# A third k-tile pair of eight goes to the 7-product scheme in the up projections of a fused encoder block

## The reference

```
h = x + 0.5 * swiglu(rms_norm(h), w_gate, w_up, w_down)       # FFN 1, hidden width 5632
...                                                           # combined projection, two attentions, gates, w_out
h = h + 0.5 * swiglu(rms_norm(h), w_gate, w_up, w_down)       # FFN 2, hidden width 5632
...                                                           # per-layer embedding, final norm
swiglu(x, wg, wu, wd) = (silu(x @ wg) * (x @ wu)) @ wd
```

## Time and profile before

| | |
|---|---|
| time, median of 3 runs | 2249.02 us (2248.64 to 2249.76) |
| profiled execution, its own time | 2249.12 us |
| span in the profile, first to last instruction | 2247.1 us |
| PE busy | 2217.0 us (99% of the span), 9950 instructions |
| DVE busy | 1337.5 us (60%) |
| ACT busy | 1050.7 us (47%) |
| DMA | 425.66 MB, mean 189 GB/s |
| mean granted TensorE clock | 0.995 |

### The profile page before, as it was taken

The page is one execution under the profiler, slowest core; times in us unless marked ns, Lnnn a source line. Parts: engine busy times, 40 slices in busy tenths (PEclk is TensorE's granted clock), DMA queues, the critical chain, the costliest instruction groups (busy, mean ns, idle before and its releaser), DMA issues.

```text
span 2247.1 us, 24310 instructions
## 1 busy us (share of the span) xinstructions
PE 2217.0 (99%) x9950; PEld 1827.4 (81%) x9950; DVE 1337.5 (60%) x1318; ACT 1050.7 (47%) x1147; POOL 40.4 (2%) x71
## 2 busy tenths in 40 slices
PE   8999999999999999999999998899999999999998
PEld 7888888888888888877778887788878888888886
DVE  5777544677555444445655654777754467755555
ACT  6445434454444444464444443454543345544454
POOL 0000000000010000010000000000000000000000
PEclk9999999999999999999999999999999999999999
DMA  8455456555465666665655664555546664556654
GB/s 312 177 202 205 164 196 205 207 186 191 175 201 187 198 195 190 175 179 173 174 168 159 187 187 143 213 172 203 207 149 191 204 221 171 197 178 212 187 189 147
DMA packets 161079, 425.66 MB, mean 189 GB/s; under 512 B 11320, under 2 KB 11328, under 8 KB 143568
## 3 DMA queue, kind: packets, MB, share of 16 engines
q1 hardware_dynamic: 159216, 419.21, 57.3%
q0 software_dynamic: 1472, 4.70, 0.8%
q10 hardware_dynamic: 288, 0.30, 0.0%
HBM read 422.06 MB, written 2.11 MB: 189 GB/s over the span
## 4 chain that ended last, share of the span: by engine, by line
PE 97%; DMA 1%; DVE 1%; ACT 0%; issue 0%; ACTq 0%; POOLq 0%; POOL 0%
PE acc L1470 18%; PE acc L1472 18%; PE acc L1471 18%; PE acc L1513 6%; PE acc L1515 6%; PE acc L1514 6%; PE turn L1515 4%; PE turn L1513 4%; PE turn L1514 4%; PE fox L1515 4%; PE fox L1514 4%; PE fox L1513 4%; DMA raw<-in_ffn_up 1%; PE turn L1490 1%; PE acc L1507 0%; PE turn L1762 0%
## 5 line engine op out<-in xcount | busy, mean ns | idle before, releaser
L1003 DVE TENSOR_TENSOR w_lo<-raw,w_hi 128x1024 fp32r<-128x1024 f32 x451 | 557.9, 1240 | 604.0 <-ACT w_hi L573 603.6
L573 ACT ACTIVATE w_hi<-raw 128x1024 fp32r<-128x1024 f32 x451 | 477.0, 1060 | 704.0 <-PE acc L1472 633.9
L1470 PE MATMUL acc<-w_hi,x_both 128*128 128x512 f32 x940 | 370.7, 394 | 2.8 <-DVE x_both L1165 2.8
L1472 PE MATMUL acc<-w_hi,x_both 128*128 128x512 f32 x940 | 366.3, 390 | 0.0
L1471 PE MATMUL acc<-w_lo,x_both 128*128 128x512 f32 x940 | 365.9, 389 | 0.0
L1470 PE MATMUL acc<-w_hi,slab_r 128*128 128x512 f32 x832 | 325.9, 392 | 2.6 <-DVE w_lo L1003 2.6
L1472 PE MATMUL acc<-w_hi,slab_r 128*128 128x512 f32 x832 | 324.5, 390 | 0.0
L1471 PE MATMUL acc<-w_lo,slab_r 128*128 128x512 f32 x832 | 324.4, 390 | 0.0
L1058 DVE TENSOR_TENSOR w_lo<-raw,w_hi 128x2048 fp32r<-128x2048 f32 x84 | 192.2, 2290 | 100.8 <-ACT w_hi L629 100.3
L629 ACT ACTIVATE w_hi<-raw 128x2048 fp32r<-128x2048 f32 x84 | 161.2, 1919 | 191.1 <-PE fox L1515 93.5
L1470 PEld LDWEIGHTS acc<-w_hi,x_both 128*128 128x128 f32 x940 | 176.5, 188 | 44.8 <-issue 5.7
(11 more groups left out here) (368 smaller groups left out, 3200.9 us busy)
## 6 DMA issues: line engine op xcount, KB each, us to landing
raw<-in_ffn_up SPq DMA_DIRECT2D x88, 1024.0 KB, 4.9
raw<-in_ffn_w_down SPq DMA_DIRECT2D x176, 512.0 KB
raw<-in_w_in SPq DMA_DIRECT2D x96, 512.0 KB
more<-in_ffn_up SPq DMA_DIRECT2D x46, 1024.0 KB, 4.9
raw<-in_w_merge_gate SPq DMA_DIRECT2D x64, 512.0 KB
raw<-in_ffn_up SPq DMA_DIRECT2D x37, 512.0 KB, 4.0
raw<-in_w_out SPq DMA_DIRECT2D x32, 512.0 KB
raw<-in_w_ple_gate SPq DMA_DIRECT2D x32, 512.0 KB
```

What stands on the lines that cost most here:

```text
L573: nc.scalar.activation(w_hi[:, slot, :, :], raw[:, slot, :, :], ACT.Copy).then_inc(hi_split, 1)
L1003: nc.vector.tensor_tensor(w_lo[:, slot, :, :], raw[:, slot, :, :], w_hi[:, slot, :, :].bitcast(F32), ALU.subtract).then_inc(lo_split, 1)
L1470: nc.tensor.matmul(to, hi(kt)[:, tok], w_hi[:, slot, k, :], start=kt == 0, stop=False)
L1472: last = nc.tensor.matmul(to, lo(kt)[:, tok], w_hi[:, slot, k, :], start=False, stop=kt == BK * nb - 1)
```

## The change

`US` goes from 2 to 3: of the eight units of a pair, three are A and B items. A middle stage now reads B0 S3 B1 S4 A0' B2 S5 A1' S6 A2' S7.

Room for it is made by sharing. Raw weights and low parts are in one ring of five buffers (`tall`: `raw` twice, `w_lo` twice, `more` once): the low part is written over the raw weights. High parts have four quads. The B tiles (`later_tiles`) are also split in place; for unit 2 they lie in `corner`, where POOL's masks and `thin_rows` lie later, and in one tile of `more`. So a raw buffer is free for a load only when PE has multiplied what was in it. The wait of L392 is gone. `make_sums` and `split_sums` go a unit at a time through `m1_copy` and `m5_copy`. `copy_parts` and `combine` stand behind the first item of a stage and no longer behind the last one of the stage before. POOL makes its masks later.

```diff
-US = 2
-QUADS = 3
+US = 3
+QUADS = 4
+TALL = 5
...
 def stage_of(pair, first, pairs):
     own = [("S", pair, u) for u in range(UNITS)]
     if pair > first:
-        own = [("B", pair, 0), own[US], ("B", pair, 1), *own[US + 1:]]
+        b0, b1, b2 = [("B", pair, u) for u in range(US)]
+        own = [b0, own[US], b1, own[US + 1], b2, *own[US + 2:]]
     if pair + 1 < pairs:
-        later = [("A", pair + 1, u) for u in range(US)]
-        own = [*own[:-2], *later, *own[-2:]]
+        a0, a1, a2 = [("A", pair + 1, u) for u in range(US)]
+        own = [*own[:4], a0, *own[4:6], a1, own[6], a2, own[7]]
     return own
...
-        quad_free, raw_free, trio_free = [b0 - 2, b0, early], [b0 - 2, b0, early], [early] * US
-        order, quad, slot, at, made = ((0, 1, 2) if name == "up2a" else (2, 0, 1)), 0, 0, b0, []
+        kinds = [kind for p in range(first, pairs) for kind, _, _ in stage_of(p, first, pairs)]
+        quads = [(i - len(kinds)) % QUADS for i in range(len(kinds))]
+        whole = UNITS * (pairs - first)
+        slots = [(r - whole) % TALL for r in range(whole)]
+        if name == "up2a":
+            quads[0], slots[0:2] = 0, (0, 1)
+        quad_free, trio_free = [b0 - 2, b0, early, early], [early] * US
+        raw_free, raw_split = [0, 0, b0 - 2, b0, early], [b0 - 2, b0, 0, 0, 0]
...
-                if up == "up2a":
-                    sp.wait_ge(multiplied, BLOCK[up])
...
-                        if it.kind != "B" and it.raw_free > 0:
-                            sp.wait_ge(lo_split, it.raw_free)
+                        if it.kind != "B":
+                            if it.raw_split > 0:
+                                sp.wait_ge(lo_split, it.raw_split)
+                            if it.raw_free > 0:
+                                sp.wait_ge(multiplied, it.raw_free)
...
                         if it.kind == "A":
-                            sp.dma_start(raw_quad(up, it.raw)[:, 0:3:2, :], source[:, 0:2, :]).then_inc(quad_full[it.raw], 16)
-                            sp.wait_ge(lo_split, it.trio_free)
-                            sp.dma_start(trio(up, it.unit)[:, 0:2, :], source[:, 2:4, :]).then_inc(trio_full[it.unit], 16)
+                            sp.dma_start(tall(up, it.raw, 0)[:, 0:3:2, :], source[:, 0:2, :]).then_inc(tall_full[it.raw], 16)
+                            sp.wait_ge(multiplied, it.trio_free)
+                            sp.dma_start(later_tiles(up, it.unit, 0)[0][:, 0:2, :], source[:, 2:4, :])\
+                              .then_inc(trio_full[it.unit], 16)
...
-                        if k == 1 and n == 0:
-                            if later_rows:
-                                later_rows()
-                            if sums is not None:
-                                make_sums(name, hi, lo, sums)
-                        if k == 3 and n == 0 and sums is not None:
-                            split_sums(sums)
+                        if k == 1 and n == 0 and later_rows:
+                            later_rows()
+                        if 2 <= k <= 4 and n == 0 and sums is not None:
+                            split_sums(k - 2, sums)
+                        if 1 <= k <= 3 and n == 0 and sums is not None:
+                            make_sums(k - 1, hi, lo, sums)
```

More of the change, by code:

```diff
@@ L49 @@
 UNITS = KD // BK
-US = 2
-QUADS = 3
+US = 3
+QUADS = 4
+TALL = 5
 DOWN_OF = {"up1a": "down1a", "up1b": "down1b", "up2a": "down2a", "up2b": "down2b"}
 BEFORE = {"up1a": "up1a", "up1b": "down1a", "up2a": "up2a", "up2b": "down2a"}
-Item = namedtuple("Item", "kind pair unit at quad quad_free raw raw_free raw_count trio_free trio_count step")
+Item = namedtuple("Item", "kind pair unit at quad quad_free raw raw_free raw_split raw_count trio_free trio_count step")
 def stage_of(pair, first, pairs):
@@ L108, in item_tables @@
 def item_tables(block):
-    counts, steps, stages, after = {"raw": [0] * QUADS, "trio": [0] * US}, 0, {}, {}
+    counts, steps, stages, after = {"raw": [0] * TALL, "trio": [0] * US}, 0, {}, {}
     for name, (pairs, first) in UPS.items():
@@ L133, in item_tables @@
                     trio_free[u] = at + 1
-                stage.append(Item(kind, pair, u, at, q, quad_free[q], raw, r_free, r_count, t_free, t_count, step))
+                stage.append(Item(kind, pair, u, at, q, quad_free[q], raw, r_free, r_split, r_count, t_free, t_count, step))
                 quad_free[q] = at + 1
@@ L138, in item_tables @@
         stages[name] = made
-        after[block[DOWN_OF[name]]] = (raw_free, quad_free)
+        split_after = [max(quad_free[n], raw_free[2 + n]) for n in range(2)]
+        after[block[DOWN_OF[name]]] = (raw_free[0:2], split_after)
     return stages, after
@@ L362, in slot_free @@
             def slot_free(blk):
-                sp.wait_ge(lo_split, raw_after(blk))
+                first = blk - blk % RING
+                if first in AFTER:
+                    sp.wait_ge(multiplied, AFTER[first][0][blk % RING // 2])
+                else:
+                    sp.wait_ge(lo_split, blk - RING + 1)
             def load(blk, src):
@@ L620, in split_item @@
             def split_item(name, it):
-                n = 3 if it.kind == "B" else 4
-                of = trio(name, it.unit) if it.kind == "B" else raw_quad(name, it.raw)
                 if it.kind == "S":
-                    act.wait_ge(quad_full[it.raw], 16 * it.raw_count)
+                    act.wait_ge(tall_full[it.raw], 16 * it.raw_count)
                 if it.kind == "A":
@@ L628, in split_item @@
                 act.wait_ge(multiplied, it.quad_free)
-                nc.scalar.activation(hi_quad(name, it.quad)[:, 0:n, :], of[:, 0:n, :], ACT.Copy)\
-                    .then_inc(hi_split, item_counts(name, it))
+                at = 0
+                for of in raw_parts(name, it):
+                    n = of.shape[1]
+                    last = nc.scalar.activation(hi_quad(name, it.quad)[:, at:at + n, :], of, ACT.Copy)
+                    at += n
+                last.then_inc(hi_split, item_counts(name, it))
             def copy_parts(name, pair):
@@ L654, in up_phase @@
                         split_item(name, it)
+                        if k == 0 and n > 0:
+                            copy_parts(name, pair)
                         if k == 1 and pair > 0:
@@ L1517, in multiply_item @@
             def multiply_item(name, it, hi, lo, primed, last_unit, ready):
-                banks, whole, rest = banks_of(name, it.pair), hi_quad(name, it.quad), lo_quad(name, it.quad)
+                banks, whole = banks_of(name, it.pair), hi_quad(name, it.quad)
+                rest = [part[:, n, :] for part in lo_parts(name, it) for n in range(part.shape[1])]
                 first, second = BK * it.unit, BK * it.unit + 1
@@ L1559, in up_groups @@
                             pe.wait_ge(turned_lo, TURN[name] + 2 * pair)
-                            if sums is not None and n == 0:
-                                pe.wait_ge(sums_lo, sums)
+                        if it.kind == "A" and sums is not None and n == 0:
+                            pe.wait_ge(sums_lo, sums - US + it.unit + 1)
                         def ready(ct):
```

162 lines of the change are left out of this document (81 added, 81 removed).

## The result

| | before | changed |
|---|---|---|
| time, median (lowest to highest), 6 runs each | 2249.39 us (2248.64 to 2249.89) | 2257.62 us (2255.91 to 2258.51) |
| profiled execution, its own time | 2249.12 us | 2255.91 us |
| span | 2247.1 us | 2253.8 us |
| mean granted TensorE clock | 0.995 | 0.998 |

The changed kernel is slower: ratio 1.0036, 95% interval 1.0025 to 1.0047. Forecast were 2243.2 us and "faster", so the time lies inside the range of 2230 to 2268, and the sign is wrong. (The profiled execution is the fastest of the changed kernel's six; between the medians +8.2 came.)

A forecast was written before the change was run, and what follows sets the result against it. The prediction took PE, holding 97% of the chain that ended last, as the bound. Its terms, -11.6 + 19.6 - 10.7 - 4.4 + 1.2 = -5.9 against 2249.1, gave 2243.2 us, range 2230 to 2268.

The forecast's parts named there:

- Matmuls: All on PE's path: 17 pairs lose 3 matmuls each, 51 at 0.2268 us, -11.6 us.
- Middle stages: 13 stages: new PE waits in front of S4 (0.65) and S6 (0.75 plus 0.1), 1.5 us each, +19.6 us.
- Landing of the second half: Middle stages: the 512 KB load of A's second half lands in 3.7 us, near bounds 3.4 and 4.1.
- slower landing: Rival, middle stages: loads issued right behind share the DMA engines, landing 4.6 to 4.9, +27, 2270 us; chance 0.17.
- The restart: Middle stages, at S6: 0.1 us extra for PE restarting without a running pipeline.
- Start of up2a: FFN 2: of 15.7 us lost before, 5.0 stays, as S0's load is issued several blocks ahead; -10.7 us.
- Turn to down2a: FFN 2: block 0's quad is free 11 us earlier, so the 4.4 us lost before go; -4.4 us.
- Start of up1a: First stage: more sums on DVE make S3 ready at 71.4 for PE at 71.0, S4 0.7 late; +1.2 us.
- the main case: The summed forecast with landing between 3.4 and 4.1, 2235 to 2254 us; chance 0.60, of it 0.03 slower.
- The clock: Rival, middle stages: each of 26 waits costs 1.8 us more in low clock, +46, 2289 us; chance 0.06.
- The loads hide: Rival, middle stages: a lone half lands by 3.2, waits cost 6.5 for 19.6, 2230 us; chance 0.13.
- It doesn't do what it says at FFN 2: Rival, FFN 2: up2a's start stays late, 2254 to 2258 us; chance 0.04.

The follow-up runs named there:

- e1: The changed kernel with B2 moved one place earlier, in front of S4, in middle stages; 2228.14 us, ratio 0.9906.
- e2: The changed kernel, but SP waits for the landing of A's second half before it issues the next load; 2250.75 us, ratio 1.0011.
- e4: The changed kernel with two units (US = 2) and the old item order, keeping the shared ring of five buffers and four quads; 2229.83 us, ratio 0.9914.
- e11: e9 with the shift by two moved to the last five raw loads of up2a, its last stage; 2224.84 us, ratio 0.9889.
- e6: The changed kernel with A's second half loaded as two DMAs of 256 KB, the second needed only by the last step; 2237.92 us, ratio 0.9952.
- e3: The changed kernel, but DVE waits for A's second half only behind the first of the four steps; 2236.48 us, ratio 0.9944.
- e7: e1 with up2a's first five raw buffers taken in the order 0 to 4; 2232.63 us, ratio 0.9931.
- e9: e1 with up2a's raw buffers numbered in order from its start and the shift by two at its last eight raw loads; 2233.94 us, ratio 0.9933.

## Why the prediction was wrong in its sign

**Matmuls, -11.6: right.** 51 fewer at an unchanged pace. PE's busy time fell by only 6.7 us, in part since what a wait costs beyond its reported length (below) counts as busy.

**Middle stages, +19.6: the mechanism right in every link, the size wrong.** Where the waits stand, how many there are, what releases them, DVE idle until a DMA lands, none at S5: all as forecast, and with the waits gone e1's stages cost nothing over their matmuls but 1.8 us in all 13. But a stage costs (44.71 - 42.38) = 2.33 us over its matmuls and transposes (43.06 less three of 0.2268) and not 1.5. Over all 13, from the transposes of one stage to those of the next, it is 29.9 us, 2.30 each, where the sum had 19.6 (13 times 1.5 is 19.5): **10.3 of the 12.7 us missed**. The terms, from the stage shown above and the landings:
- *Landing of the second half, taken as 3.7.* This is the step that failed. The 3.65 was worked out for a lone load, and e2 measures 3.6 for a lone one (3.76 in the mean of all 26). In the kernel the load isn't alone: the prediction wrote that SP's queue "holds nothing else then", which is true of what stands in front, and left out what stands behind. The mean landing in the middle stages is 3.99: 26 times 0.29 is 7.5 us. The followers account for 0.23 of each 0.29, the difference to e2's mean. The rival "slower landing" named just this mechanism (the S load and A half issued 0.4 and 0.8 us behind) and had it at 4.6 to 4.9, too dear. Its reason against, that the first halves had a follower and took 4.0, was itself the right price: 4.0 was the median of a 512 KB load with followers, and with 4.0 in place of 3.7 the prediction's own slope (10.4 us for 0.4) gives +7.8, 2251.0, "no change".
- *Rounding and hops.* By the prediction's own figures the waits are 0.7 and 0.8 (11.0 less 10.3, 11.0 less 10.2); it wrote 0.65 and 0.75. And B0 to S4 less the landing is 7.34 (11.22 - 3.88), where its terms give 7.31. Together 0.08 to 0.09 a wait in the stage shown, 2.2 us for 26.
- *The restart: right.* From the first matmul behind a wait to the second is 0.34 (164.03 to 164.37), 0.11 more than the pace. At S4 it was there before without a wait, behind the transposes (157.08 to 157.40), so only S6's is new, and the sum had 0.1 for it.

```profile
157.08 0.48 PE L1513 MATMUL turn<-w_hi,x_both 128*128 128x512 f32 x1
157.40 0.40 PE L1514 MATMUL turn<-w_lo,x_both 128*128 128x512 f32 x1
```

These add up to 9.7, against 10.3 measured. By the landing alone the forecast would have been 2250.7; the rounding and the starts of up2a and up1a (below) make most of the rest.

**Start of up2a, -10.7: -8.9 came.** From the end of out to the transposes of the second stage PE lost 15.8 us before and loses 6.9 now. The first load was issued at 1393.86, before the end of out, and PE waited 1.07 at S2 and 3.62 at S3 (5.2 against the pace), where the sum said 1.1 and 3.7 (22.1 less 18.4), put at 5.0 in all. What it left out is the clock behind the longer wait: granted 0.72 in the 6.1 us behind 1430.90, where matmuls stand 0.43 us apart. The prediction held that a wait of 3.0 us had cost no clock there, and didn't ask it of one of 3.6. PE's timeline:

```profile
1421.51 0.50 PE L1533 MATMUL acc<-more_r,y_r 128*128 128x512 f32 x1 [1.07 <-DVE more_r L1078]
...
1430.90 0.50 PE L1533 MATMUL acc<-w_hi,y_r 128*128 128x512 f32 x1 [3.62 <-DVE raw_r L1078]
```

The ten steps behind 1430.90 take 3.99 us, seven of them 0.43, where 2.27 would be the pace: 1.7 us. That is the term that the sum left out, and nearly all of the 1.8 missed here.

**Turn to down2a, -4.4: right.** No wait and no low clock; the matmuls go on at 0.227 us across the turn, which answers to the earlier trace rows:

```profile
1680.33 0.39 PE L1535 MATMUL fox<-more_r,y_r 128*128 128x512 f32 x1
1680.56 0.39 PE L1490 MATMUL acc<-w_hi,slab_r 128*128 128x512 f32 x1
```

e4 adds the two FFN 2 terms up: -18.8 by the traces (-19.1 by the medians), where 15.7 and 4.4 less one wait of 1.1 make -19.0.

**Start of up1a, +1.2: the waits in their places, 1.95 came.** Two waits, 0.36 at 71.20 and 1.07 at 78.01; the sum had S3 ready at 71.4 for a PE at 71.0, and S4 0.7 late. The stage lasts 1.95 us longer than its matmuls and transposes, 0.7 over the sum. With 10.3 and 1.8 that makes 12.8; in front of up1a's transposes the changed kernel is 0.3 us ahead, which no term had. So the 12.7 are accounted for within 0.2.

**Why the sign turned.** The net was the difference of two large terms, -26.7 and +20.8. The larger part of the miss is an error of 8% in one load's time (3.99 for 3.7), repeated 26 times: 7.5 us, more than the net. The chances (0.28 for slower) said as much, but the main case gave only 0.03 of its 0.60 to slower, though its own upper end was 2254.

**The rivals.** *The clock* did not come in the stages: 26 short waits in 13 stages with a granted clock of 1.00. The Trainium skill, "TensorE: Matmul & The Clock Gate", section "A second HAM failure mode: psum-queue depth-cycling", says that frequent micro-idles between matmul groups can make the clock oscillate; at two waits of 0.5 to 1.6 us in 44 us these traces show none of it. *The loads hide* did not come: no 512 KB load on the chain landed under 3.43, e2's lone ones included. The Trainium skill, "DMA: Bandwidth & Descriptors", section "Anatomy of one DMA", gives 3.2 by its fit for the path that GpSimd issues; the runs here (issued by SP) show 3.6 alone and 4.0 with followers, and the measurement decides. *Slower* is the one that came, by its mechanism, at 4.0 and not at 4.6. *It doesn't do what it says at FFN 2* fell with 1393.86.

## What to carry to other kernels

When buffers are shared so that a load waits for the consumer, the way from freeing through load, preparation and split to the next use becomes a loop, and each tenth of a microsecond in it is paid at every turn: lay it out from the trace, price its load with the loads that will be issued right behind it, and place the freeing item early enough to have a margin larger than the uncertainty (here the order of one item was worth 29.5 us, and left 0.4 us of margin at S6). A wait should stand in front of the first instruction that needs it, not of the group. Renumbering buffers moves a shortage rather than removing it, unless the shift lands where no A unit is loaded (e11). And time each part of a change alone: here the part made only for room gained 19 us, and the part that the change was for lost 28 as it was placed.

## What the runs showed of the hardware

- *Loads issued behind slow the one in front.* 512 KB to 128 partitions, by SP, in middle stages without a packet of an instruction queue meanwhile: 3.59 us alone (e2), 3.88 with 1 MB issued 0.4 us later on the same queue (behind B0's also 512 KB, 0.8 us later). With such a packet: 4.14 and 4.22.
- *Half the bytes save a fifth.* 256 KB pieces took 3.21 us in the mean with followers (2.84 to 3.75, e6), 512 KB 3.99.
- *A wait of PE costs more than the profile's number for it.* The reported wait starts at the modelled end of the last matmul or transpose. In the stage shown, 0.65 and 0.81 are reported, while against the pace PE lost 0.92 and 0.97 (164.03 less 152.81 and 10.3; 183.53 less 172.36 and 10.2), and 0.11 more at the restart behind the second. Over all 26, PE lost 29.9 us and 22.3 are reported: 0.3 us on top of each.
- *Clock behind a wait in up2a.* Waits of 1.76 (e11), 2.89 (e3) and 2.98 us (before) were followed by a granted clock of 1.00 in the next 6 us; those of 3.25 (e6), 3.62 (changed), 3.69 (e1), 6.77 (e7) and 7.58 us (e9) by 0.72, 0.72, 0.51, 0.58 and 0.71. In down2a of the kernel before, a wait of 2.6 already went with 0.79, and one of 1.79 at 6.76 in e1 with 0.72, so length alone doesn't settle it; what else does is open.
